# Earlier sums for two pairs of gate weights, two products moved between attention steps, head transposes moved behind both pairs

## The reference, cut to what matters

```python
hm = rmsnorm(mlstm(...), mlstm_norm_w) * sigmoid(o_m)          # 512 x 512
# differential attention, 4 heads, query blocks of 128
p = softmax(q_d @ k_d.T * scale)          # two maps per head
a = p[:, :, 0] - lam * p[:, :, 1]
hd = rmsnorm(a @ v_d, subln_w) * (1.0 - lam_init)              # 512 x 512
merged = sigmoid(g_m) * (hm @ w_br_m) + sigmoid(g_d) * (hd @ w_br_d)
x = x + gate1 * (merged @ w_out)
h2 = rmsnorm(x, norm2_w) * (1.0 + scale2) + shift2
x = x + gate2 * hierarchical_moe(h2, ...)                      # 32 experts
```

## Time and profile before

| | us |
|---|---|
| median of three runs | 1344.81 |
| the profiled execution | 1335.61 |
| its span | 1333.7 |
| PE busy | 1226.0 (92%) |
| DVE busy | 567.9 |
| ACT busy | 307.7 |
| POOL busy | 245.7 |

### The profile page before, as it was taken

One profiled execution on the slowest core, in us unless ns is written; L12 is line 12 of the kernel. 1 busy time (PEld: TensorE's weight loads), 2 busy tenths in 40 slices (PEclk: granted clock), 3 DMA queues, 4 the chain that ended last, 5 costly groups with the idle time before them and its releaser, 6 DMA issues.

```text
span 1333.7 us, 13264 instructions
## 1 busy us (share of the span) xinstructions
PE 1226.0 (92%) x4904; PEld 682.6 (51%) x4904; DVE 567.9 (43%) x1436; ACT 307.7 (23%) x725; POOL 245.7 (18%) x214
## 2 busy tenths in 40 slices
PE   7999989999989999999999998799999789877785
PEld 3454434445544444688864456577664534332331
DVE  3204483467557741229952377422223522311221
ACT  3313653433210001231032344200011211110110
POOL 7000022354500000072300003212200022111100
PEclk9999999999989999999999899899999989988888
DMA  9525122323365521403330202202257589999993
GB/s 326 108 71 126 63 83 45 111 71 136 106 209 184 195 93 66 158 1 127 127 126 1 64 1 64 68 1 63 64 220 300 205 325 408 402 408 404 407 362 90
DMA packets 92679, 213.01 MB, mean 160 GB/s; under 512 B 20234, under 2 KB 51226, under 8 KB 80792
## 3 DMA queue, kind: packets, MB, share of 16 engines
q1 hardware_dynamic: 79088, 190.98, 39.1%
q0 software_dynamic: 10176, 17.96, 5.5%
q10 hardware_dynamic: 3344, 3.16, 0.7%
HBM read 205.69 MB, written 14.75 MB: 165 GB/s over the span
## 4 chain that ended last, share of the span: by engine, by line
PE 68%; SPq 12%; DVE 9%; DMA 4%; ACT 3%; issue 2%; POOL 0%; POOLq 0%; DVEq 0%; ACTq 0%
SPq L2727 10%; PE PS L2243 6%; PE PS L966 6%; PE PS L1381 4%; PE PS L1459 4%; PE PS L2302 4%; PE PS L1642 4%; PE PS L1644 4%; PE PS L2410 3%; PE PS L611 3%; PE PS L2842 3%; PE PS L1688 2%; PE PS L1390 2%; PE PS L1700 2%; PE PS L681 2%
## 5 line engine op out<-in xcount | busy, mean ns | idle before, releaser
L966 PE MATMUL PS<-HT,W 128*128 128x512 f32 x256 | 126.0, 616 | 1.8 <-ACT AN L1130 1.7
L1228 POOL TENSOR_SCALAR AN<-AN,SM 128x128 f32<-128x128 f32 (+3 forms) x64 | 72.2, 1135 | 202.7 <-DVE SM L1320 202.7
L2842 PE MATMUL PS<-AN,HT 128*64 128x512 f32 x272 | 84.8, 639 | 17.3 <-DMA AN<-in_w_up 8.4
L1251 DVE SCALAR_TENSOR_TENSOR AN<-AN,COLA 128x256 f32<-128x256 f32 x168 | 85.1, 507 | 5.0
L611 PE MATMUL PS<-W,HT 128*128 128x512 f32 (+1 forms) x192 | 72.2, 538 | 0.0
L2921 DVE TENSOR_TENSOR HT<-HT,PS 128x256 f32<-128x256 f32 x16 | 6.7, 421 | 151.1 <-ACT HT L2899 151.1
L966 PEld LDWEIGHTS PS<-HT,W 128*128 128x128 f32 x256 | 45.0, 195 | 39.7 <-issue 36.1
L2842 PEld LDWEIGHTS PS<-AN,HT 128*64 128x64 f32 x272 | 27.9, 148 | 70.5 <-issue 68.5
L1381 PE MATMUL PS<-HT,W 128*128 128x512 f32 x128 | 58.1, 599 | 0.0
L2410 PE MATMUL PS<-W,AN 128*128 128x512 f32 x128 | 57.6, 597 | 0.0
L1459 PE MATMUL PS<-W,AN 128*128 128x512 f32 x128 | 55.5, 593 | 1.9 <-DVE GBC L1265 1.9
(11 more groups left out here) (507 smaller groups left out, 2240.0 us busy)
## 6 DMA issues: line engine op xcount, KB each, us to landing
W<-in_w_in SPq DMA_DIRECT2D x14, 2048.0 KB, 8.6
W<-in_w_down SPq DMA_DIRECT2D x20, 1024.0 KB, 23.5
AN<-in_w_ada SPq DMA_DIRECT2D x17, 1024.0 KB, 5.3
AN<-in_w_gate SPq DMA_DIRECT2D x15, 1024.0 KB, 19.0
AN<-in_w_up SPq DMA_DIRECT2D x15, 1024.0 KB, 27.1
AN<-in_w_down SPq DMA_DIRECT2D x12, 1024.0 KB, 21.3
W<-in_w_gate SPq DMA_DIRECT2D x10, 1024.0 KB, 24.9
W<-in_w_up SPq DMA_DIRECT2D x10, 1024.0 KB, 28.8
```

Of the source, the lines that this page charges most:

```text
L966: t = pe.matmul(u.ap, w[:, c, tile(m)], hT[:, c, :], start=c == 0, stop=c == 7)
L1228: pool.tensor_scalar(PU[u % 5][:, 0:n], PU[u % 5][:, 0:n], RSUM[:, u:u + 1], None, ALU.mult).then_inc(*sc_pool.up(u))
L1251: dve.scalar_tensor_tensor(out=a, in0=wt[:, c, :], scalar=ca["c2"][:, c:c + 1], in1=a, op0=ALU.mult, op1=ALU.add).then_inc(*ada_dve.up(p, c))
L2842: t = pe.matmul(u.ap[r, :].rearrange("p (n f) -> p n f", n=2), XGT[e % 2][:, c, r], w_gu(3 * e + half)[:, c], start=c == 0, stop=c == 7)
```

## The change

Three things move; no arithmetic is added or dropped.

1. The sums of g = 0 go to other tiles, `WS0`: KM for n = 0 and QM for n = 1. POOL waits only for "mqk" (3, 3) and for the weights. The sums of g = 1 now wait for what g = 0 waited for, and for the last multiplication of hd ("hd", 3), but no longer for product 4 of pairs (0, 0) and (0, 1).
2. Products 1 and 2 of pair (0, 0) are issued in steps 16 and 17 of `pe_diff`, ahead of the transposes there.
3. PE turns hm behind pair (0, 1), directly ahead of hd, and DVE copies it out behind pair (0, 1).

```diff
+    WS0 = [[a[:, x, :].rearrange("p (c f) -> p c f", c=4) for x in range(3)] for a in (KM, QM)]
...
                 pe_om(pe, wp, step)
+            elif step < ND + 2:
+                pe_gate_product(pe, wp, 0, 0, step - ND + 1)
...
-                s1, s2, s4 = WS[n]
+                s1, s2, s4 = gate_sums(g, n)
                 wg.wait_ge(*ring[2 + g % 2].at("g2", g))
-                if g:
-                    wg.wait_ge(*B.use("prod", g - 1, n, 4).full)
-                else:
+                if g == 0:
+                    wg.wait_ge(*B.use("mqk", 3, 3).full)
+                elif g == 1:
                     wg.wait_ge(*B.use("dpT", ND - 1).full)
                     wg.wait_ge(*B.use("dacc", 3).full)
                     wg.wait_ge(*diff_dve.at("p", ND - 1))
+                    wg.wait_ge(*om_dve.at("hd", 3))
+                else:
+                    wg.wait_ge(*B.use("prod", g - 1, n, 4).full)
...
+    def pe_gate_pair(pe, wp, g, n):
+        for x in ((6, 5, 7, 3, 4) if (g, n) == (0, 0) else (1, 2, 6, 5, 7, 3, 4)):
+            pe_gate_product(pe, wp, g, n, x)
...
             pe_gate_pair(pe, wp, g, 0)
+            pe_gate_pair(pe, wp, g, 1)
             if g == 0:
                 for i in range(NT):
                     pe_turn_h(pe, wp, "hmT", HM, i, om_dve.at("gated", i))
-            pe_gate_pair(pe, wp, g, 1)
-            if g == 0:
-                for i in range(NT):
                     pe_turn_h(pe, wp, "hdT", HD, i, om_dve.at("hd", i))
...
         dve_gate_pair(dve, wd, 0, 0)
-        dve_turn_hm(dve, wd)
...
             dve_gate_pair(dve, wd, g, 1)
             if g == 0:
+                dve_turn_hm(dve, wd)
                 gated(g, 0)
```

More of the change, by code:

```diff
@@ L2227, in pool_halves, with gate_sums, pe_gate_product @@
                 step((g, n, 4), pool.tensor_tensor(s4, a12, s2, ALU.subtract))
-    def pe_gate_pair(pe, wp, g, n):
+    def gate_sums(g, n):
+        return WS[n] if g else WS0[n]
+    def pe_gate_product(pe, wp, g, n, x):
         a11, a12, a21, a22 = gate_w(g, n)
         b11, b12, b21, b22 = half_t
-        s1, s2, s4 = WS[n]
+        s1, s2, s4 = gate_sums(g, n)
+        s, t = {1: (a11, b11), 2: (a12, b21), 6: (s2, TS[1]), 5: (s1, TS[0]), 7: (a21, TS[2]), 3: (s4, b22),
+                4: (a22, TS[3])}[x]
+        u = B.take(0, 6, "prod", g, n, x)
+        wp.wait_ge(*u.free)
         wp.wait_ge(*ring[2 + g % 2].at("g2", g))
         wp.wait_ge(*win2_pool.at("T", 4))
[L2236 to L2244, removed]
+        if x in (6, 5, 7, 3):
+            wp.wait_ge(*win_pool.at(g, n, {5: 1, 6: 2, 7: 3, 3: 4}[x]))
+        for c in range(4):
+            m = pe.matmul(u.ap[:, 0:256], s[:, c, :], t[:, c, :], start=c == 0, stop=c == 3)
+        m.then_inc(*u.filled)
+    def pe_gate_pair(pe, wp, g, n):
+        for x in ((6, 5, 7, 3, 4) if (g, n) == (0, 0) else (1, 2, 6, 5, 7, 3, 4)):
+            pe_gate_product(pe, wp, g, n, x)
     def act_gate_pair(act, wa, g, n):
```

## The result

The changed kernel runs in 1326.07 us (median of four, 1325.4 to 1330.87), the kernel before in 1343.0 (median of four); the ratio is 0.9883 with a 95% interval of 0.984 to 0.9926. In a second comparison on one chip it was 0.9921 (0.9894 to 0.9948), 1327.43 against 1338.83. The forecast was 1333.

The account below looks back on a forecast made before the run. PE was taken to bound the stretch, starved by DVE, whose multiplications POOL's sums slowed. Branch products 13.4 us earlier less 1.7 for early sums gave 11.7, off the median of 1344.81: 1333, range 1325 to 1341.

Parts of the forecast that it names:

- The brake: DVE's 16 multiplications L2036, behind the attention: free of POOL's sums they take 4.3 us in place of 15.75.
- The early sums: POOL's sums of g = 0 moved into the first attention steps: stalls of DVE make PE 1.7 us late.
- The products between the steps: Products 1 and 2 of pair (0, 0) among the last attention steps: values end about 819.4, last transposes 0.9 us later.
- The turned heads: Transposes of hm and hd behind both pairs: 5.4 us for 4.2 of work, a new wait of 1.2 us.
- The rest moves along: Behind the branch products: experts' transfers, released by the last merged-branch sum, start and end that much earlier.
- The sum: Whole kernel: 13.4 us gained less 1.7 lost is 11.7; off the median of 1344.81 that gives 1333.1.
- costlier sums: Rival, first attention steps: DVE stalls reach PE at 7.0 us, gain only 6.4, total 1338; chance 0.12.
- L2036 slow for another reason: Rival, DVE's 16 multiplications: something other than POOL holds them, gain about 3.5 us, total 1341; chance 0.05.
- time that comes back: Rival, experts' stream of transfers: held by something that does not move, total 1345; chance 0.05.
- slower: Rival, attention's start: eight stalls of 1.35 us and two clock falls put it 3.2 us over, total 1348; chance 0.04.

Follow-up runs that it names:

- late_sums: Changed kernel with the sums of g = 0 held back until the attention's end; 0.9937 of the kernel before, scores to branch product 93.2 us against 88.3 in the change.
- second_sums_beside: Changed kernel with the sums of g = 1 not waiting for hd's multiplications, free to run beside L2037; 0.9965 of the kernel before, scores to branch product 96.0 us.
- pool_reads_beside: Changed kernel plus eight POOL additions reading SBUF right behind the attention; one run 1334.07 us against 1337.94 before, scores to branch product 97.2 us.
- pool_writes_beside: Changed kernel plus 16 POOL memsets, which read no SBUF, right behind the attention; one run 1325.66 us against 1337.94 before, scores to branch product 88.3 us.
- part 3 alone: Kernel before with only hm's transposes and copies moved behind both pairs; 0.9996 of the kernel before, scores to branch product 99.2 us against 100.6.
- paced_sums: Changed kernel with the eight sums of g = 0 issued one per attention step, each behind that step's difference; 0.9907 of the kernel before, scores to branch product 86.7 us.
- products_behind: Changed kernel with products 1 and 2 of pair (0, 0) back behind the attention; 0.9927 of the kernel before, scores to branch product 92.5 us.

## Why the prediction was right, by its steps

- **The brake.** L2036 held by POOL's sums: shown, by the profile after and from three sides (late_sums, second_sums_beside, pool_reads_beside), and its kind by pool_writes_beside. 4.3 us were forecast, 4.29 measured; DVE's end at 825.8 plus the early 1.7, measured 826.75. The slack behind it is smaller than I had it. I looked at the second bank of pair (0, 1), free by 827; the first is the one that counts. It holds product 2, which DVE reads from 827.54 to 827.95, and PE needs it at 828.83: 0.9 us in hand.
- **The early sums.** 1.7 us were forecast, 53.01 - 51.36 = 1.65 measured, with the last arrival 0.75 us later than I took it (757.15 for 756.4). The stalls are three, on the smallest instructions too; DVE's timeline, with the POOL instruction on which the first stall ends:

```profile
758.49 1.26 POOL L2231 TENSOR_TENSOR AN<-AN,W 128x512 f32<-128x512 f32 x1
758.60 1.17 DVE L1982 TENSOR_TENSOR SM<-SM 128x1 f32<-128x1 f32 x1 [1.01 <-ACT SM L1953]
...
764.76 0.38 DVE L2128 SCALAR_TENSOR_TENSOR SM<-SM 128x1 f32<-128x1 f32 x1
765.18 1.43 DVE L2130 SCALAR_TENSOR_TENSOR AN<-AN,SM 128x128 f32<-128x128 f32 x1
```

  against 0.16, 0.22 and 0.35. The way to PE was another than I wrote: not the transpose of the first difference waited, but the scores, for banks that ACT's exponentials held (L2065, 0.46 and 0.40 us). Within two groups of scores there are another 0.34 us each (0.83 for 0.49). That the size came out so close is in part luck. I had the first difference 3.3 us late, and with 1.6 us of slack that made 1.7. It was 2.3 us late (766.61 less 764.54, with first scores 0.19 us earlier), which by my way would have cost 0.7; the banks made the rest. In the six traces with early sums the cost was 0.95 to 1.7 us.
- **The products between the steps.** The order is as forecast; the attention's values ended 0.9 us earlier than I had them (820.19 for the start of what follows, where 819.4 plus 1.7 stood). For 0.5 us of it that is because I had taken a group of transposes and values at 1.6 and 2.6 us, with the ends that the trace models, and from start to start they are 1.33 and 2.34.
- **The turned heads.** 5.4 us were forecast, 846.61 - 840.91 = 5.7 measured. Here I misread the edit, and the description of the change has it so too: hm's and hd's units alternate, one each per turn of one loop, they do not stand in two blocks. So each of the two banks belongs to one copying engine, and the pace is PE's unit with its way to DVE, 0.75 us, and DVE's copy, 0.69, together 1.44 us for two units (the next copy starts at 844.43):

```profile
842.99 0.69 DVE L2045 TENSOR_TENSOR AN<-PS,COLB 128x512 f32<-128x512 f32 x1 [0.75 <-PE PS L2008]
```

- **The rest moves along.** The first expert weights are asked for at 976.36 instead of 988.82, 12.46 us earlier, as forecast. From there to the end this pair of traces gives 2.3 us back, within the 4 us by which the eleven traces differ there; the whole times, 11.4 and 17 us apart, show no more coming back than that.
- **The sum.** 11.7 us forecast, 12.3 by the ruler. The 1326 of the result lies lower than 1333 mostly because the median of 1344.81, from which I subtracted, was high: 29 runs on one chip gave 1340.16 and eleven on another 1338.83, and there the change was 11.4 us faster. So the 7 us between forecast and result lie in the starting point; the gain itself was 0.6 us off by the ruler. Differences between the medians of a few runs, 17 in the first comparison, are no measure of a gain of 12.

Of the rivals, costlier sums (7.0), L2036 slow for another reason, time that comes back, and slower all fall. Parts 1 and 2 are worth 4.9 and 4.2 us when taken from the whole and part 3 alone 1.4; they do not add up to 12.3, since a wait that one part takes away can stand behind another.

## What to carry to other kernels

The remedy is that of paced_sums: look for DVE instructions that take several times as long as the shortest of the same line, and lay POOL's timeline beside them. If the long ones pass one per POOL instruction and have both inputs in SBUF, move POOL's reads to where DVE reads at most one input from SBUF, one at a time behind the DVE instruction that has just finished. Moving the transposes, which is what the page of the profile pointed to by the longest wait, gave 1.4 us alone by one trace each, and no change of the whole time; the engine that the wait named was late for another engine's sake. And where executions drift by more than a change is worth, measure between two instructions that enclose it, in more than one trace of each kernel.

## What the runs showed of the hardware

A DVE instruction of 128 x 1 elements with both inputs in SBUF took 1.17 us instead of 0.16 beside POOL's additions. It began at 758.60 and ended at 759.77, where POOL's addition, begun at 758.49, ended at 759.75; the next one (L2128) ended at 765.14, with an addition that ended at 765.13. So a small instruction pays what is left of POOL's instruction, 1.0 us in the one case and 0.16 in the other, and in products_behind, where it fell between two additions, it paid nothing. POOL itself lost nothing by it: its additions took 1.26 to 1.28 us and followed at 1.35, with DVE's multiplications beside them and without. POOL memsets of 128 x 512 (16 in 9.25 us) cost DVE nothing. And a wait of 1.91 us on PE was followed by a lower granted clock in one profile (0.83 from 824.6 to 834.6 us, in products_behind) and not in another with the same waits (1.00 from 816 to 826 us, in the kernel before).
